# Reading the moving weights of the token-major products from the last column to the first

## The chip, the core and the metric

The kernel runs on one core of one Trainium2 chip. The time is that of the device for one execution of the whole program, in microseconds. The other cores of the chip have no work.

## What is computed

Two transformer blocks run one after the other on an activation `x` of 256 tokens by 2048 features, all in float32. Each block has a mixer and a feed-forward part. The attention and the recurrence are cut here, because the change touches none of their instructions.

```python
def first_block(x, ...):
    h = rms_norm(x, pre_mix_norm)
    proj = h @ w_in                       # 2048 x 5656
    mix = attention_of(proj)              # differential heads and compressed, selected and windowed heads
    x = x + rms_norm(mix @ w_out, post_mix_norm)
    h = rms_norm(x, pre_ffn_norm)
    u = causal_dwconv(h @ w_up, conv_w, conv_b)          # 2048 x 11264
    gate, up = jnp.split(u, 2, axis=-1)
    y = (jax.nn.gelu(gate, approximate=True) * up) @ w_down   # 5632 x 2048
    return x + rms_norm(y, post_ffn_norm)

def second_block(x, ...):
    proj = rmsnorm(x, mix_pre_gain) @ w_in_2             # 2048 x 5376
    mixed = concatenate([window_attention(proj), recurrence(proj)]) @ w_out_2
    x = x + rmsnorm(mixed, mix_post_gain)
    u = relu(rmsnorm(x, mlp_pre_gain) @ w_up_2)          # 2048 x 8192
    return x + rmsnorm((u * u) @ w_down_2, mlp_post_gain)
```

## The kernel before

Every large matrix product streams its weights from HBM once. A tile of weights is 512 KB, 128 partitions by 1024 float32 columns. SyncE brings it into one of eight slots of `stage`. ScalarE copies it to `whi` (lines 732, 790, 983, 1134), which rounds it to the type float32r, and VectorE subtracts that from the original and writes the rest to `wlo` (lines 1198, 1226, 1629, 1837). Both have four slots. The activations are kept in the same two parts, high in columns 0 to 255 and low in columns 256 to 511 of each chunk of 128 features. A product is the sum of three partial ones: high by high, high by low and low by high.

A matmul of TensorE holds a stationary operand of 128 by 128 in the array and streams a moving operand past it, one column after the other. Each column of the moving operand makes one column of the output in PSUM. The kernel has two kinds of products:

- **Feature-major** (`in1` and `in2` in part, `up1a`, `up1b`, `up2a`, `up2b`; lines 2097 and 2100, 2368 and 2371, 2024 and 2028): the weights are stationary, the activations move. The output has features on its partitions.
- **Token-major** (`in1` and `in2` in part, `out1`, `out2`, `down1a`, `down1b`, `down2a`, `down2b`): the activations are stationary, and the weights move. The output has 128 tokens on its partitions and up to 512 features in a bank of PSUM. The three partial products of one chunk follow each other, `ah` by `h`, `ah` by `l`, `al` by `h`, all into the same bank. They are lines 1911 to 1913 in `chunk`, 2113 to 2115 in `tok_tile`, and 2381 to 2383 in `in2_tile`. In most of them a weight tile holds two chunks of 512 columns (`NW`); some blocks of the input projections are 256 or 280 columns wide.

TensorE waits with `lo_done` until VectorE has written the whole of a tile of `wlo`, and gives the slot back with `tile_used` after the last matmul that reads it. So neither of these semaphores knows in which order the columns of a tile are read. Sixteen chunks of 128 rows make one sum for an input or output projection; the down projections sum over more. The order of all products is written out by hand in the program of each engine, and no planner moves anything.

On the host, `kernel` hands each input to the program as it is.

Of the kernel before, what the change touches and what calls it, by code (L numbers as in the profile page):

```python
# [17 lines left out]
D = 2048  # L18
S = 256
TT = S // P  # L20
KC = D // P
# [32 lines left out]
NW = 512  # L54
TC = TILE // NW
# [5 lines left out]
IN2_BLOCKS = [("tok", C_KA, 256)] + [("feat", C_QA + 256 * i, 256) for i in range(4)]  # L61
for _i in range(4):
# [13 lines left out]
IN1_BLOCKS = [("feat", C_KC, 256), ("feat", C_VC, 256), ("feat", C_KS, 256), ("feat", C_KW, 256),  # L76
              ("tok", C_VS, 256), ("feat", C_NQ, 256), ("tok", C_VW, 256 + GATES)]
# [48 lines left out]
def in2_block(n):  # L126

    k = max(k for k in range(len(IN2_BLOCKS)) if IN2_FIRST[k] <= n)
    return k, n - IN2_FIRST[k]
# [74 lines left out]
def build(nc, w, out, scratch, roots):  # L204
# [4 lines left out]
    def ev(name):  # L209

        if name not in sems:
            sems[name] = ctx.enter_context(nc.semaphore(name))
        return sems[name]

    with ctx:
# [81 lines left out]
        spans = win[:, 2048:4096]  # L297
# [135 lines left out]
        def region1_width(n):  # L433

            if n >= IN1_TILES:
                return TILE
            kind, _, wd = IN1_BLOCKS[in1_block(n)[0]]
            return TILE if kind == "feat" else TC * wd
# [54 lines left out]
        def _(sp):  # L493
# [5 lines left out]
            def tok_block(name, i, b, base):  # L499

                m, k0 = WT[name]
                col, _, _, wd = place(name, i, b)
                for j in range(G[name].tiles):
                    k = k0 + TC * j
                    slot = (b * G[name].tiles + j) % STAGES
                    tile_in(slot, base + j, m[k * P:(k + TC) * P, span(col, wd)].rearrange("(c p) n -> p c n", p=P),
                            stage[:, slot, 0:TC * wd].rearrange("p (c n) -> p c n", c=TC))
# [1396 lines left out]

        @block.tensor
        def _(pe):
            def chunk(o, lhs, k, s, c, t, ends):

                h, l = whi[:, s, c * NW:(c + 1) * NW], wlo[:, s, c * NW:(c + 1) * NW]
                ah, al = lhs[:, k, t * P:(t + 1) * P], lhs[:, k, S + t * P:S + (t + 1) * P]  # L1910
                nc.tensor.matmul(o, ah, h, start=k == 0, stop=False)  # L1911
                nc.tensor.matmul(o, ah, l, start=False, stop=False)  # L1912
                return nc.tensor.matmul(o, al, h, start=False, stop=ends and c == TC - 1)  # L1913

            def held_tiles(name, lhs, base):

                T = G[name].tiles
                for t in range(TT):
                    for j in range(T - HELD, T):
                        if t == 0:  # L1920
                            pe.wait_ge(ev("lo_done"), base + (j + 1 + STAGES))
                        for c in range(TC):
                            last = chunk(PS[:, LAST_BANK[name] + t, :], lhs, TC * j + c, (base + j) % SPLITS, c, t, j == T - 1)
                        if t == 1:
                            last.then_inc(ev("tile_used"), 1)
                    if t == 0:
                        last.then_inc(ev("half_tile"), 1)
# [26 lines left out]
            def last_chunks(turn):  # L1954

                n = {"n2": 0, "n3": 1, "n4": 2}[turn]
                pe.wait_ge(ev("actlo_" + turn), 4)
                turn_chunks(turn, range(12, KC))
                pe.wait_ge(ev("resid"), PIECES * n + 6)
                turn_chunks(turn, range(12, KC), t=1)  # L1960
# [144 lines left out]
            def tok_tile(bank, s, wd, first):  # L2105

                for c in range(TC):
                    at_k = first + c
                    h, l = whi[:, s, c * wd:(c + 1) * wd], wlo[:, s, c * wd:(c + 1) * wd]
                    for t in range(TT):  # L2110
                        o = PS[:, bank + t, 0:wd]
                        ah, al = act1[:, at_k, t * P:(t + 1) * P], act1[:, at_k, S + t * P:S + (t + 1) * P]
                        nc.tensor.matmul(o, ah, h, start=at_k == 0, stop=False)  # L2113
                        nc.tensor.matmul(o, ah, l, start=False, stop=False)  # L2114
                        last = nc.tensor.matmul(o, al, h, start=False, stop=at_k == KC - 1)  # L2115
                return last

            def out1_here(n):

                b, q = out1_tile(n)  # L2120
                if q == 0:
                    if b == 0:
                        pe.wait_ge(ev("in1_join"), len(IN1_FEAT))
                    if b == 1:
                        pe.wait_ge(ev("in1_tok"), 2 * len(IN1_TOK))
                    if b == 3:
                        pe.wait_ge(ev("actlo_mix1"), KC)
                    if b == 2:
                        pe.wait_ge(ev("diff_o"), HD)
                        pe.wait_ge(ev("actlo_mix1"), HN + 4)  # L2130
                if b < 2:
                    pe.wait_ge(ev("actlo_mix1"), TC * (q + 1))
                pe.wait_ge(ev("lo_done"), n + 1 + STAGES)
                tok_tile(2 * (b % 2) + 4 * (b // 2), n % SPLITS, NW, TC * q).then_inc(ev("tile_used"), 1)
# [209 lines left out]
            def in2_tile(n):  # L2344

                k, j = in2_block(n)
                kind, _, wd = IN2_BLOCKS[k]
                banks, s = IN2_BANKS[k], n % SPLITS
                if j == 0 and k == 14:
                    pe.wait_ge(ev("in2_join"), FEAT_NO[12] + 1)  # L2350
                elif j == 0 and k > 14:
                    pe.wait_ge(ev("in2_tok"), 2 * TOK_NO[k - 2] + 2)
                elif k < 14 and j == 0 and k >= 2:
                    if k - 2 in FEAT_NO:
                        pe.wait_ge(ev("in2_join"), FEAT_NO[k - 2] + 1)
                    else:
                        pe.wait_ge(ev("in2_tok"), 2 * TOK_NO[k - 2] + 2)
                if k == 0 and j == 2:
                    last_chunks("n3")
                if k == 0:  # L2360
                    pe.wait_ge(ev("actlo_n3"), TC * (j + 1))
                pe.wait_ge(ev("lo_done"), G["in2"].first + n + 1 + STAGES)
                if kind == "feat":
                    for c in range(FC):
                        at_k = FC * j + c
                        for f in range(2):
                            o, at = PS[:, banks[f], :], slice(c * FW + f * P, c * FW + (f + 1) * P)
                            nc.tensor.matmul(o, whi[:, s, at], act2[:, at_k, :], start=at_k == 0, stop=False)  # L2368
                        for f in range(2):
                            o, at = PS[:, banks[f], :], slice(c * FW + f * P, c * FW + (f + 1) * P)  # L2370
                            last = nc.tensor.matmul(o[:, S:2 * S], wlo[:, s, at], act2[:, at_k, 0:S], start=False, stop=at_k == KC - 1)  # L2371
                else:
                    for t in range(TT):
                        if t == 1 and j == 0 and k >= 14:
                            pe.wait_ge(ev("in2_tok"), 2 * TOK_NO[k - 1] + 1)
                        for c in range(TC):
                            at_k = TC * j + c
                            h, l = whi[:, s, c * wd:(c + 1) * wd], wlo[:, s, c * wd:(c + 1) * wd]
                            o = PS[:, banks[t], 0:wd]
                            ah, al = act2[:, at_k, t * P:(t + 1) * P], act2[:, at_k, S + t * P:S + (t + 1) * P]  # L2380
                            nc.tensor.matmul(o, ah, h, start=at_k == 0, stop=False)  # L2381
                            nc.tensor.matmul(o, ah, l, start=False, stop=False)  # L2382
                            last = nc.tensor.matmul(o, al, h, start=False, stop=at_k == KC - 1)  # L2383
                        if t == 0 and j == 7 and k >= 13:
                            last.then_inc(ev("first_half"), 1)
                last.then_inc(ev("tile_used"), 1)
# [161 lines left out]
        "mlp_pre_gain_2", "mlp_post_gain_2", "w_up_2", "w_down_2"]  # L2548


# [19 lines left out]
```

## Time and profile before

| | us |
|---|---|
| median of three runs | 2238.51 |
| lowest and highest run | 2238.21, 2238.97 |
| span of the profiled execution | 2235.6 |
| TensorE matmul busy | 2215.5 (99%) |
| TensorE weight load busy | 1891.4 (85%) |
| VectorE busy | 1416.2 (63%) |
| ScalarE busy | 1118.0 (50%) |

The span goes from the first to the last instruction of the profiled execution. It is 2.9 us shorter than the median of the runs, and no device time beside its span is recorded for that execution itself. In the profile, matmuls are pipelined and their ends are modelled: two of them overlap in the trace, so the duration of one says less than the distance from the start of one to the start of the next. Where this text speaks of a matmul's spacing, it is that distance.

### The profile page before, as it was taken

Reading aid. Unit: us, or ns where it says so; the run is one execution under the profiler, and the core shown is the slowest. Engines: PE = TensorE matmul, PEld = TensorE weight load, DVE = VectorE, ACT = ScalarE, POOL = GpSimd, SP = SyncE. Lnnn points to the kernel's source line nnn. Section 1 sums busy time; section 2 is a strip of 40 time slices with the busy share of each in tenths; the row PEclk is TensorE's granted clock in tenths of the full one; section 3 lists DMA queues with packets and bytes.
Section 4 is the critical chain, followed back from the end, with each engine's and each line's share of the span. In section 5 each row is a group of like instructions: output and inputs, shape, how many; then the busy total and the mean of one; then the engine's idle time right before and its main releaser. Section 6 shows DMA issues by size and latency. Waiting matters only on the chain.

```text
span 2235.6 us, 34152 instructions
## 1 busy us (share of the span) xinstructions
PE 2215.5 (99%) x12721; PEld 1891.4 (85%) x12721; DVE 1416.2 (63%) x1827; ACT 1118.0 (50%) x1567; POOL 65.7 (3%) x95
## 2 busy tenths in 40 slices
PE   8999999999999999999999999999999999999998
PEld 7888888888888888888888888888888888888887
DVE  6466685677776447777566786657666444666545
ACT  5454464555555445555454554545444444444443
POOL 5100000000000000000000000000000000000000
PEclk9999999999999999999999999999999999999999
DMA  9954455566566666666657455566666666666663
GB/s 291 317 180 133 132 167 181 162 190 205 178 201 195 190 194 189 187 188 200 209 147 206 142 162 160 180 195 167 196 191 193 191 196 190 191 192 188 214 192 112
DMA packets 321663, 418.84 MB, mean 187 GB/s; under 512 B 13566, under 2 KB 233048, under 8 KB 320788
## 3 DMA queue, kind: packets, MB, share of 16 engines
q1 hardware_dynamic: 316548, 398.81, 58.3%
q0 software_dynamic: 4720, 16.49, 2.5%
q10 hardware_dynamic: 288, 2.10, 0.3%
q8 instruction: 69, 1.13, 0.2%
q14 instruction: 38, 0.31, 0.0%
HBM read 414.85 MB, written 2.49 MB: 187 GB/s over the span
## 4 chain that ended last, share of the span: by engine, by line
PE 95%; DVE 2%; DMA 1%; issue 1%; ACT 1%; POOL 0%; POOLq 0%; DVEq 0%; SPq 0%; ACTq 0%
PE PS L2024 25%; PE PS L2028 13%; PE PS L1912 10%; PE PS L1911 10%; PE PS L1913 10%; PE PS L2097 5%; PE PS L2368 3%; PE PS L2100 2%; PE PS L2113 2%; PE PS L2115 2%; PE PS L2114 2%; PE PS L2371 2%; PE PS L2381 1%; PE PS L2383 1%; PE PS L2382 1%
## 5 line engine op out<-in xcount | busy, mean ns | idle before, releaser
L2024 PE MATMUL PS<-actu,whi 128*128 128x512 f32 x2432 | 755.6, 392 | 0.0
L2028 PEld LDWEIGHTS PS<-actu,wlo 128*128 128x128 f32 x2432 | 457.1, 188 | 99.9
L1226 DVE TENSOR_TENSOR wlo<-stage,whi 128x1024 fp32r<-128x1024 f32 x296 | 360.4, 1223 | 216.5 <-ACT whi L790 216.2
L1198 DVE TENSOR_TENSOR wlo<-stage,whi 128x1024 fp32r<-128x1024 f32 x245 | 298.9, 1225 | 301.2 <-ACT whi L732 301.2
L2028 PE MATMUL PS<-actu,wlo 128*128 128x256 f32 x2432 | 480.0, 279 | 0.0
L790 ACT ACTIVATE whi<-stage 128x1024 fp32r<-128x1024 f32 x296 | 311.4, 1057 | 304.9 <-PE PS L2028 291.6
L732 ACT ACTIVATE whi<-stage 128x1024 fp32r<-128x1024 f32 x245 | 258.7, 1060 | 344.6 <-PE PS L1913 321.4
L2024 PEld LDWEIGHTS PS<-actu,whi 128*128 128x128 f32 x2432 | 368.4, 188 | 0.6 <-issue 0.4
L1913 PE MATMUL PS<-whi,gT 128*128 128x512 f32 x864 | 336.4, 389 | 0.0
L1912 PE MATMUL PS<-wlo,gT 128*128 128x512 f32 x864 | 336.4, 389 | 0.0
L1911 PE MATMUL PS<-whi,gT 128*128 128x512 f32 x864 | 336.4, 389 | 0.0
L1629 DVE TENSOR_TENSOR wlo<-stage,whi 128x1024 fp32r<-128x1024 f32 (+2 forms) x125 | 145.3, 1166 | 109.0 <-ACT whi L983 108.7
L983 ACT ACTIVATE whi<-stage 128x1024 fp32r<-128x1024 f32 (+2 forms) x125 | 125.8, 1010 | 150.0 <-PE PS L2100 79.8
L1911 PEld LDWEIGHTS PS<-whi,gT 128*128 128x128 f32 x864 | 162.3, 188 | 33.8
L1913 PEld LDWEIGHTS PS<-whi,gT 128*128 128x128 f32 x864 | 162.2, 188 | 33.6
L1912 PEld LDWEIGHTS PS<-wlo,gT 128*128 128x128 f32 x864 | 162.2, 188 | 33.2
L2097 PE MATMUL PS<-act,whi 128*128 128x512 f32 x512 | 164.5, 403 | 0.0
L1837 DVE TENSOR_TENSOR wlo<-stage,whi 128x1024 fp32r<-128x1024 f32 (+1 forms) x86 | 102.9, 1204 | 62.4 <-ACT whi L1134 61.8
L1134 ACT ACTIVATE whi<-stage 128x1024 fp32r<-128x1024 f32 (+1 forms) x86 | 89.3, 1044 | 90.0 <-PE PS L2371 45.6
L2368 PE MATMUL PS<-act,whi 128*128 128x512 f32 x384 | 122.5, 400 | 0.1
L2100 PEld LDWEIGHTS PS<-act,wlo 128*128 128x128 f32 x512 | 96.3, 188 | 22.6
L2100 PE MATMUL PS<-act,wlo 128*128 128x256 f32 x512 | 101.0, 279 | 0.0
(338 smaller groups left out, 2482.4 us busy)
## 6 DMA issues: line engine op xcount, KB each, us to landing
stage<-in_w_up SPq DMA_DIRECT2D x304, 512.0 KB, 3.9
stage<-in_w_down SPq DMA_DIRECT2D x216, 512.0 KB, 4.2
stage<-in_w_in SPq DMA_DIRECT2D x160, 512.0 KB, 3.8
stage<-in_w_out SPq DMA_DIRECT2D x64, 512.0 KB, 4.2
stage<-in_w_in SPq DMA_DIRECT2D x16, 256.0 KB, 4.0
DQK<-in_cmp_k_w POOLq DMA_DIRECT2D x8, 512.0 KB, 6.6
DQK<-in_cmp_v_w POOLq DMA_DIRECT2D x8, 512.0 KB, 6.3
stage<-in_w_in SPq DMA_DIRECT2D x8, 280.0 KB, 8.3
```

Of the source, the lines that this page charges most:

```text
L732: nc.scalar.activation(whi[:, s % SPLITS, 0:wd], stage[:, s % STAGES, 0:wd], ACT.Copy)\
L790: nc.scalar.activation(whi[:, j % SPLITS, :], stage[:, j, :], ACT.Copy).then_inc(ev("hi_done"), 1)
L1198: nc.vector.tensor_tensor(wlo[:, s % SPLITS, 0:wd], stage[:, s % STAGES, 0:wd], whi[:, s % SPLITS, 0:wd].bitcast(F32), ALU.subtract).then_ ...
L1226: nc.vector.tensor_tensor(wlo[:, j % SPLITS, :], stage[:, j, :], whi[:, j % SPLITS, :].bitcast(F32), ALU.subtract).then_inc(ev("lo_done"), 1)
L1911: nc.tensor.matmul(o, ah, h, start=k == 0, stop=False)
L1912: nc.tensor.matmul(o, ah, l, start=False, stop=False)
L1913: return nc.tensor.matmul(o, al, h, start=False, stop=ends and c == TC - 1)
L2024: nc.tensor.matmul(o, whi[:, j % SPLITS, at], actu[:, k, :], start=k == 0, stop=False)
L2028: last = nc.tensor.matmul(o[:, S:2 * S], wlo[:, j % SPLITS, at], actu[:, k, 0:S], start=False, stop=k == KC - 1)
L2097: nc.tensor.matmul(o, whi[:, s, at], act1[:, at_k, :], start=at_k == 0, stop=False)
L2100: last = nc.tensor.matmul(o[:, S:2 * S], wlo[:, s, at], act1[:, at_k, 0:S], start=False, stop=at_k == KC - 1)
L2368: nc.tensor.matmul(o, whi[:, s, at], act2[:, at_k, :], start=at_k == 0, stop=False)
```

## The change

In the three places where weights move, the moving operand is now given with a step of minus one: the access pattern starts at the last column of the chunk and runs to the first. So that each output column still lands where it did, the host turns round the order of the columns of each block in the weight matrices. Column 511 of a chunk in SBUF now holds what column 0 held. The outputs in PSUM are written from column 0 upwards, as before. In `w_in` and `w_in_2` only the token-major blocks are turned; `w_up` and `w_up_2` are left as they are.

```diff
+            def falling(ap):
+
+                return ap[:, ::-1]
+
             def chunk(o, lhs, k, s, c, t, ends):
...
-                nc.tensor.matmul(o, ah, h, start=k == 0, stop=False)
-                nc.tensor.matmul(o, ah, l, start=False, stop=False)
-                return nc.tensor.matmul(o, al, h, start=False, stop=ends and c == TC - 1)
+                nc.tensor.matmul(o, ah, falling(h), start=k == 0, stop=False)
+                nc.tensor.matmul(o, ah, falling(l), start=False, stop=False)
+                return nc.tensor.matmul(o, al, falling(h), start=False, stop=ends and c == TC - 1)
...
+def moving_last_first(name, a):
+
+    if name in ("w_out", "w_out_2", "w_down", "w_down_2"):
+        spans = [(at, at + NW) for at in range(0, D, NW)]
+    elif name in ("w_in", "w_in_2"):
+        spans = [(col, col + wd) for kind, col, wd in (IN1_BLOCKS if name == "w_in" else IN2_BLOCKS) if kind == "tok"]
+    else:
+        return a
+    a = a.copy()
+    for at, end in spans:
+        a[:, :, at:end] = a[:, :, at:end][:, :, ::-1].copy()
+    return a
...
-        a = np.ascontiguousarray(inputs[name])
+        a = moving_last_first(name, np.ascontiguousarray(inputs[name]))
```

`tok_tile` and the token-major branch of `in2_tile` are edited like `chunk`. The sequence of instructions on every engine, their sizes, their waits and all transfers are the same before and after; the program gives each of these matmuls as one instruction, as before. The output arrays and their layout are unchanged.

## Rows read from the trace of the kernel before

**Rows 1.** The page: span, busy time by engine, granted clock and DMA in 40 slices.
```profile
span 2235.6 us, 34152 instructions
PE 2215.5 (99%) x12721; PEld 1891.4 (85%) x12721; DVE 1416.2 (63%) x1827; ACT 1118.0 (50%) x1567; POOL 65.7 (3%) x95
...
PEclk9999999999999999999999999999999999999999
DMA  9954455566566666666657455566666666666663
...
PE 95%; DVE 2%; DMA 1%; issue 1%; ACT 1%; POOL 0%; POOLq 0%; DVEq 0%; SPq 0%; ACTq 0%
```

**Rows 2.** Waits of TensorE: whom it waited for, us in total, times, longest us.
```profile
PE PS L2049 <- DMA ident<-const_ident: 6.6, 1, 6.6
PE PS L1934 <- DVE x L1360: 3.3, 5, 1.1
```

**Rows 3.** Groups by line and shape: count, busy us, mean ns, idle before us.
```profile
L1911 PE MATMUL PS<-whi,gT 128*128 128x512 f32 x864 | 336.4, 389 | 0.0
L2113 PE MATMUL PS<-whi,act 128*128 128x512 f32 x176 | 69.7, 396 | 0.0
L1911 PE MATMUL PS<-whi,act 128*128 128x512 f32 x144 | 56.2, 390 | 0.0
L2381 PE MATMUL PS<-whi,act 128*128 128x512 f32 x128 | 50.9, 398 | 0.0
L2113 PE MATMUL PS<-whi,act 128*128 128x280 f32 x32 | 9.6, 298 | 0.0
L2113 PE MATMUL PS<-whi,act 128*128 128x256 f32 x32 | 9.3, 289 | 0.0
L2381 PE MATMUL PS<-whi,act 128*128 128x256 f32 x32 | 9.2, 289 | 0.3 <-DVE act L1323 0.3
```

**Rows 4.** Timeline of TensorE in a token-major stage: start us, duration us, instruction.
```profile
754.74 0.39 PE L1911 MATMUL PS<-whi,gT 128*128 128x512 f32 x1
754.97 0.39 PE L1912 MATMUL PS<-wlo,gT 128*128 128x512 f32 x1
755.19 0.39 PE L1913 MATMUL PS<-whi,gT 128*128 128x512 f32 x1
...
757.91 0.39 PE L1913 MATMUL PS<-whi,gT 128*128 128x512 f32 x1
```

**Rows 5.** Timeline of TensorE in the 280-column block of the first input projection.
```profile
94.43 0.29 PE L2113 MATMUL PS<-whi,act 128*128 128x280 f32 x1
...
96.50 0.29 PE L2114 MATMUL PS<-wlo,act 128*128 128x280 f32 x1
```

**Rows 6.** Timeline of TensorE around a product of plain float32 operands (L2237).
```profile
182.53 0.59 PE L2237 MATMUL PS<-work,VS 128*128 128x256 f32 x2
182.96 0.38 PE L2238 MATMUL PS<-work,VS 128*128 128x128 f32 x2
```

**Rows 7.** Lines 2450 and 2467: duration ns min/median/max, first and last start us.
```profile
L2450 PE MATMUL PS<-win x128: 218/219/244, 1335.4 to 1337.2; 128*32 128x64 f32 x128
...
L2467 PE MATMUL PS<-win x32: 221/222/270, 1377.4 to 1378.3; 128*64 128x64 f32 x32
```

**Rows 8.** Timelines of ScalarE and VectorE in down2a, with the idle time before each.
```profile
1751.56 1.06 ACT L732 ACTIVATE whi<-stage 128x1024 fp32r<-128x1024 f32 x1 [1.66 <-PE PS L1913]
...
1752.66 1.23 DVE L1198 TENSOR_TENSOR wlo<-stage,whi 128x1024 fp32r<-128x1024 f32 x1 [1.50 <-ACT whi L732]
1755.38 1.23 DVE L1198 TENSOR_TENSOR wlo<-stage,whi 128x1024 fp32r<-128x1024 f32 x1 [1.50 <-ACT whi L732]
```

**Rows 9.** Stage by window, down2a: engines' busy us (count), granted clock, DMA share, GB/s.
```profile
1702.40:1876.30 173.90, 173.90 (x770) 144.08 (x769) 82.89 (x68) 72.62 (x72) 0.00 (x0) 1.00 0.63 193
```

**Rows 10.** DMA issues: count, KB each, median us from issue to landing.
```profile
stage<-in_w_down SPq DMA_DIRECT2D x216, 512.0 KB, 4.2
```

**Rows 11.** Timeline of TensorE in a feature-major stage.
```profile
1000.16 0.62 PE L2024 MATMUL PS<-actu,whi 128*128 128x512 f32 x2
1000.62 0.40 PE L2028 MATMUL PS<-actu,wlo 128*128 128x256 f32 x2
1000.85 0.62 PE L2024 MATMUL PS<-actu,whi 128*128 128x512 f32 x2
```

More of the change, by code:

```diff
@@ L2112, in tok_tile @@
                         ah, al = act1[:, at_k, t * P:(t + 1) * P], act1[:, at_k, S + t * P:S + (t + 1) * P]
-                        nc.tensor.matmul(o, ah, h, start=at_k == 0, stop=False)
-                        nc.tensor.matmul(o, ah, l, start=False, stop=False)
-                        last = nc.tensor.matmul(o, al, h, start=False, stop=at_k == KC - 1)
+                        nc.tensor.matmul(o, ah, falling(h), start=at_k == 0, stop=False)
+                        nc.tensor.matmul(o, ah, falling(l), start=False, stop=False)
+                        last = nc.tensor.matmul(o, al, falling(h), start=False, stop=at_k == KC - 1)
                 return last
@@ L2380, in in2_tile @@
                             ah, al = act2[:, at_k, t * P:(t + 1) * P], act2[:, at_k, S + t * P:S + (t + 1) * P]
-                            nc.tensor.matmul(o, ah, h, start=at_k == 0, stop=False)
-                            nc.tensor.matmul(o, ah, l, start=False, stop=False)
-                            last = nc.tensor.matmul(o, al, h, start=False, stop=at_k == KC - 1)
+                            nc.tensor.matmul(o, ah, falling(h), start=at_k == 0, stop=False)
+                            nc.tensor.matmul(o, ah, falling(l), start=False, stop=False)
+                            last = nc.tensor.matmul(o, al, falling(h), start=False, stop=at_k == KC - 1)
                         if t == 0 and j == 7 and k >= 13:
```

## The prediction

> **What bounds the kernel now.** I read the page first, then the waits of TensorE, then the groups by line and shape, then the timelines of single stages. The page gives TensorE 99% busy and 95% of the chain that ended last, at a granted clock of 9 tenths or more in all 40 slices [rows 1]; in the stage that I look at most closely it is 1.00, so the level of 2.4 GHz [rows 9]. TensorE waited 6.6 us once for the first transfer, and then hardly again: the next entry of its list is 3.3 us in five waits [rows 2]. So no engine feeds it too slowly, and the time is the sum of the spacings of its matmuls. A change to the matmuls' own speed reaches the end one to one, and nothing else does.
>
> The token-major products are 4,224 matmuls. Lines 1911 to 1913 have 864 + 144 each, so 3,024 in all; lines 2113 to 2115 have 176 + 32 + 32 each, so 720; lines 2381 to 2383 have 128 + 32 each, so 480 [rows 3]. Of these 3,936 are 512 columns wide (3 x 864, 3 x 176, 3 x 144 and 3 x 128), 96 are 280 wide and 192 are 256 wide.
>
> Their spacing is very regular. From 754.74 to 757.91 us lie 14 spacings, so one is 226.4 ns [rows 4]. At 2.4 GHz 512 columns take 213.3 ns, which leaves 13.1 ns per matmul. For 280 columns, 16 spacings fill 94.43 to 96.50 us, so 129.4 ns against 116.7 ns: 12.7 ns are left [rows 5]. In a feature-major stage two matmuls of 512 and two of 256 columns take 1000.85 - 1000.16 = 0.69 us [rows 11], against 1,536 columns / 2.4 = 640 ns: 12.5 ns per matmul. So a matmul of this type costs its columns at full rate plus about 13 ns, whichever operand moves and however wide it is. Of the span, token-major products fill 3,936 x 0.2264 + 96 x 0.1294 + 192 x 0.120 (256 / 2.4 + 13 ns) = 891 + 12 + 23 = 926 us, or 41%. The other 59% is not touched.
>
> **The change, part by part.**
>
> *Data and transfers.* The host turns the columns in DRAM, the tiles have the same shape and size, and a weight tile lands in 4.2 us as before [rows 10]. The copy to `whi` and the difference for `wlo` work column by column, and don't care what a column holds. Cost: none. The numbers that TensorE multiplies are the same, only in other places of SBUF.
>
> *Waits.* TensorE now begins a tile with the column that was written last. But it waits for the whole tile of `wlo`, and so no semaphore has to move. The cover is ample too: in down2a VectorE works 1.23 us and then idles 1.50 us for each tile, ScalarE works 1.06 and idles 1.66 us [rows 8], and the DMA engines are 63% busy [rows 9]. Nothing is released earlier or later, because the last matmul on a slot is the same one. Cost: none.
>
> *The step of minus one on 4,224 moving operands.* This is the whole question, and the trace of before has no operand that is read downwards. So I bound it on both sides by the nearest rows.
>
> Towards the gain, the most that can vanish is the part of a spacing that is not columns: 13 ns x 4,224 = 55 us, for a total of 2183.5. I see no reason why the direction should remove it. The feature-major matmuls pay the same 12.5 ns with quite other operands, and it doesn't depend on the width.
>
> Towards the loss, there are two prices. One is a fixed cost at each start, if the address has to be set up in another way or the first line is fetched too late to hide. The nearest size for that is what a start costs today, 13 ns once more: 55 us. The other is a lower rate. The trace has a row for a stream that takes its columns at half the rate: line 2237 multiplies plain float32, and its two records of 256 columns take 182.96 - 182.53 = 0.43 us, 0.215 us each [rows 6], which is 0.84 ns a column. If a downward read fell to this rate, a matmul of 512 columns would take 0.43 us, 0.204 more: x 3,936 = 803 us. The 96 of 280 columns would take 0.235 instead of 0.129 (10 us more), the 192 of 256 0.215 instead of 0.120 (18 us more). Together 831 us, and a total of 3069.
>
> What do other rows say of unusual moving operands? Line 2450 moves 64 columns that lie in two pieces of 32, far apart in SBUF, and line 2467 moves 64 columns in one piece. The two-piece records last 219 ns, the one-piece ones 222 ns [rows 7]. A break of the address in the middle of a stream costs nothing that can be seen. And in the 280-column block the second chunk starts at column 280 of the tile, the first at column 0, and all the spacings are alike [rows 5]. These rows are the nearest to the change: where a stream begins and where it jumps doesn't matter. They don't show a negative step, and line 2450 runs at the half rate of plain float32, so they would not show an access that is only good for half of the full rate. I take 0 ns per matmul, and keep 13 ns more as the end of the likely cases.
>
> The Trainium skill, in "Advanced Engine Details and Errata", section "Memory Cachelines", says that SBUF has lines of 16 bytes, and that a stream with at least two hits on each line has its full rate. Four-byte columns read downwards hit each line four times, as upwards; by that rule the sum is unchanged at 2238.5, and the half rate doesn't come. No run here shows the rule for a falling read of TensorE.
>
> *The writes to PSUM.* They rise as before and go to the same banks, three partial products in a row to one bank. If they fell in one matmul and rose in the next, the last column written would be needed at once; here nothing of that kind changes. Cost: none.
>
> The sum is 2235.6 + 0 for the profiled execution; its span lies 2.9 us under the median of the runs, and with these the forecast is 2238.5.
>
> **The rivals.**
>
> *A start that costs more (slower).* If each falling stream needs a few ns more before its first column, at each of the 4,224 matmuls, it reaches the end in full, since TensorE is never late for anything else. The price is 4.2 us for each nanosecond: 2242.7 with 1 ns, 2293.5 with 13 ns. It decides against "no change" from 1.1 ns (4.5 us, 0.2% of the time). For it speaks that starts aren't free today. Against it, the evenness of the spacings whatever the start and whatever the width.
>
> *Half rate (slower).* 3069, as worked out above. For it speaks that the full rate moves four bytes per column at 2.4 GHz, while plain float32 is served at half of that; a port that reads two neighbouring columns at once would do so only upwards, if it was built simply. Against it: a fetch of aligned pairs or lines serves either direction. The price decides from any loss of rate above 0.5% of the columns' time (4.5 us of the 891).
>
> *The start gets cheaper (faster).* If the 13 ns are the wait for the first columns of a rising stream, and a falling one avoids that, up to 55 us go: 2183.5. From 1.1 ns on it can be measured. VectorE and ScalarE would keep up, with 1.5 us idle in a tile that would be 12 x 13 ns = 0.16 us shorter [rows 8]. Against it speaks that the moving activations and the moving weights pay the same.
>
> The Trainium skill, in "TensorE: Matmul & The Clock Gate", section "Back-to-back issue gap", gives columns / 2.4 + 2.5 ns for a single matmul's gap, so 215.8 ns for 512 columns. The row shows 226.4, so the trace disagrees by 10.6 ns; were the falling read to reach the page's gap, 4,224 x 10.6 = 45 us would go, for 2194.
>
> *The change doesn't do what it says.* Turned data read in turned order might be made into a rising read somewhere, and then the time is that of before. In the program each of these matmuls has a moving operand with the step -1, so I count this with "no change", and give it no chance of its own.
>
> **How the numbers follow.** No change 0.64; a dearer start 0.14; half rate 0.12; a cheaper start 0.10. The predicted time is that of the likeliest, 2238.5. Its own range is 2234 to 2243, about 0.2% each way, which is what a measurement of this kernel can tell from no change. For 8 in 10 the range takes in the dearer start up to one more start of today's size (2293.5, rounded up to 2296) and the small part of a cheaper start down to 2230 (2 ns per matmul). Half rate, at 3069, and the rest of the cheaper start stay outside, some 0.2. Faster by over 0.2%: 0.10. Within 0.2%: 0.64. Slower: 0.14 + 0.12 = 0.26.
>
> **What would show it.** In the profile of the changed kernel, the spacing of lines 1911 to 1913 would stay at 226 ns, and down2a would fill 173.9 us [rows 9]. A dearer start shows as the same addition to 256, 280 and 512 columns; a lower rate shows as an addition that grows with the width. Feature-major stages must keep their 0.69 us for four matmuls, and TensorE's list of waits must stay as short as it is. If VectorE or ScalarE had other durations on the token-major tiles, my step on the data would be wrong. If TensorE's granted clock left 1.00, something outside of this argument would be at work.

## The result: 24 us slower, all of it in the 512-column products

| | before | after |
|---|---|---|
| median us | 2238.36 (4 runs) | 2262.77 (4 runs) |
| lowest and highest run | 2238.06, 2238.97 | 2262.17, 2263.38 |
| span of the profiled execution | 2235.6 | 2260.5 |

The ratio is 1.0109, with a 95% interval of 1.0095 to 1.0123. The change costs 24.4 us. That lies inside the range, but "no change" was wrong.

The page of the kernel after, first, with the lines that answer to [rows 1]:

```profile
span 2260.5 us, 34152 instructions
PE 2240.4 (99%) x12721; PEld 1890.3 (84%) x12721; DVE 1417.0 (63%) x1827; ACT 1119.2 (50%) x1567; POOL 65.8 (3%) x95
...
PEclk9999999999999999999999999999999999999999
```

TensorE is busy 24.9 us longer, and the span grew by 24.9 us. VectorE and ScalarE have what they had, the counts of instructions are the same, and the granted clock did not move. TensorE's waits, for [rows 2], stay small too: 5.8 us for the first transfer, and at most 2.8 us in total for any other entry.

```profile
PE PS L2053 <- DMA ident<-const_ident: 5.8, 1, 5.8
PE PS L1938 <- DVE x L1360: 2.8, 5, 0.9
```

The stages tell where the time went. This is down2a by window, for [rows 9], and the feature-major stage up2b behind it:

```profile
1717.10:1896.20 179.10, 179.10 (x770) 144.32 (x769) 82.86 (x68) 72.75 (x72) 0.00 (x0) 1.00 0.62 188
1896.30:2072.90 176.60, 176.60 (x1025) 155.42 (x1024) 110.48 (x92) 82.08 (x80) 0.00 (x0) 1.00 0.64 190
```

down2a takes 179.1 us in place of 173.9, so 5.2 us or 6.8 ns for each of its 768 matmuls. up2b has this row before:

```profile
1876.50:2053.00 176.50, 176.50 (x1024) 155.46 (x1023) 110.45 (x92) 81.95 (x80) 0.00 (x0) 1.00 0.63 190
```

So the feature-major stage is untouched. The timeline of TensorE in the kernel after, in a down stage, is to be read beside [rows 4]:

```profile
755.12 0.40 PE L1917 MATMUL PS<-whi,gT 128*128 128x512 f32 x1
755.36 0.40 PE L1915 MATMUL PS<-whi,gT 128*128 128x512 f32 x1
755.59 0.40 PE L1916 MATMUL PS<-wlo,gT 128*128 128x512 f32 x1
...
757.92 0.40 PE L1917 MATMUL PS<-whi,gT 128*128 128x512 f32 x1
```

Twelve spacings fill 2.80 us: 233.3 ns each, where 226.4 was read before, alike for all three lines. But in the 256-column block the spacing is no longer than it was. These rows are of the kernel after, then of the kernel before:

```profile
65.73 0.28 PE L2118 MATMUL PS<-wlo,act 128*128 128x256 f32 x1
...
66.92 0.28 PE L2119 MATMUL PS<-whi,act 128*128 128x256 f32 x1
```

```profile
65.74 0.28 PE L2114 MATMUL PS<-wlo,act 128*128 128x256 f32 x1
...
66.94 0.28 PE L2115 MATMUL PS<-whi,act 128*128 128x256 f32 x1
```

Ten spacings: 1.19 us after, 1.20 before. So it is not one addition per start. Nor is it a loss of rate in proportion to the columns: that would put some 3.4 ns on a 256-column matmul, half of the 6.9 at 512. Whatever it is depends on the width in another way. Summed over all starts in the two traces, the 3,936 spacings at 512 columns come to 25.0 us more, 6.4 ns each; the 96 at 280 columns to 0.1 us more and the 192 at 256 columns to 0.2 us less. That is the 24.9 us of the span.

### The profile page after: what moved, and what is told of

The parts are those of the page before. It is cut to its first block, busy times and chain, and to the rows that moved or that the text cites. A ratio compares the mean times of both kernels' runs of the same rounds, so it can differ in the third digit from the quotient of the medians.

```text
span 2260.5 us, 34152 instructions
## 1 busy us (share of the span) xinstructions
PE 2240.4 (99%) x12721; PEld 1890.3 (84%) x12721; DVE 1417.0 (63%) x1827; ACT 1119.2 (50%) x1567; POOL 65.8 (3%) x95
## 4 chain that ended last, share of the span: by engine, by line
PE 95%; DVE 2%; DMA 1%; issue 1%; ACT 1%; POOL 0%; POOLq 0%; DVEq 0%; ACTq 0%
PE PS L2028 25%; PE PS L2032 12%; PE PS L1915 10%; PE PS L1917 10%; PE PS L1916 10%; PE PS L2101 5%; PE PS L2372 3%; PE PS L2104 2%; PE PS L2117 2%; PE PS L2118 2%; PE PS L2119 2%; PE PS L2375 2%; PE PS L2385 1%; PE PS L2386 1%; PE PS L2387 1%
## 5 line engine op out<-in xcount | busy, mean ns | idle before, releaser
L1226 DVE TENSOR_TENSOR wlo<-stage,whi 128x1024 fp32r<-128x1024 f32 x296 | 360.4, 1224 | 215.8 <-ACT whi L790 215.5
L1916 PE MATMUL PS<-wlo,gT 128*128 128x512 f32 x864 | 343.4, 397 | 0.0
L1915 PE MATMUL PS<-whi,gT 128*128 128x512 f32 x864 | 343.3, 397 | 0.0
L1917 PE MATMUL PS<-whi,gT 128*128 128x512 f32 x864 | 343.3, 397 | 0.0
```

Source lines behind the costliest of these rows:

```text
L1226: nc.vector.tensor_tensor(wlo[:, j % SPLITS, :], stage[:, j, :], whi[:, j % SPLITS, :].bitcast(F32), ALU.subtract).then_inc(ev("lo_done"), 1)
L1915: nc.tensor.matmul(o, ah, falling(h), start=k == 0, stop=False)
L1916: nc.tensor.matmul(o, ah, falling(l), start=False, stop=False)
L1917: return nc.tensor.matmul(o, al, falling(h), start=False, stop=ends and c == TC - 1)
```

## The experiments

### One part alone: the data, and one matmul of three

```diff
 # e1_data_only: the columns stay turned on the host
-                return ap[:, ::-1]
+                return ap
```

> The kernel after with the columns turned on the host and the moving operands read upwards as in the kernel before, so that the token-major outputs come out in turned order. Theory A, B and C (the cost sits in the direction of the read): 2238.4 us, as before, spacing 226.4 ns. Theory D (the turned data, by other values next to each other, cost the 24.4 us): 2262.8.

Measured: 2237.69 us (10 runs), beside 2237.73 for the kernel before; ratio 1.0001, interval 0.9992 to 1.0011. The turned data cost nothing that can be measured here, so theory D is out. The cost sits in the direction of the read.

```diff
 # e2_low_falls: in the three places, against the kernel after
-                nc.tensor.matmul(o, ah, falling(h), start=k == 0, stop=False)
+                nc.tensor.matmul(o, ah, h, start=k == 0, stop=False)
                 nc.tensor.matmul(o, ah, falling(l), start=False, stop=False)
-                return nc.tensor.matmul(o, al, falling(h), start=False, stop=ends and c == TC - 1)
+                return nc.tensor.matmul(o, al, h, start=False, stop=ends and c == TC - 1)
```

> The kernel after with only the second of the three matmuls (the one that moves wlo) read downwards; the first and third read upwards. The columns of the high and low part then don't fit each other, which leaves the sums of the token-major products wrong, with the same instructions. Theory A: a third of the cost, 8.1 us, so 2246.5, and only the matmul that falls has the longer spacing. If the cost sits in the turn from one direction to the other rather than in the direction, two of three spacings carry it: 2254.6 or more. If it sits in falling after falling, nothing is left: 2238.4.

Measured: 2245.62 us against 2237.73, ratio 1.0034 (1.0020 to 1.0048). That is 7.9 us, a third of 24.4. By the starts in its trace, in the products with `gT`, the falling matmul has a mean of 232.5 ns to the next start, and the two rising ones 226.7 and 227.6. So it is the falling matmul's own cost, not one of changing the direction.

### Widths, directions and traffic in a program of its own

A small program shows what a whole kernel hides. It loads four tiles, splits them as the kernel does, and then TensorE runs one block of 96 matmuls after another, each on a line of its own:

```python
# 512 down
for r in range(8):
    for c, t in ((0, 0), (0, 1), (1, 0), (1, 1)):
        for k, (a, m) in enumerate(trio(512, c, t, r, 0)):   # (ah, h), (ah, l), (al, h)
            nc.tensor.matmul(PS[:, t, 0:512], a, down(m), start=k == 0, stop=k == 2)
```

> A program of its own: it loads 4 tiles, splits them in the high and low part as the kernel does, and then TensorE alone runs blocks of 96 matmuls in the order of a token-major tile (high, low, high), one block on each source line, widths 64 to 512, rising and falling, and some at 512 with other patterns. The attention, the products and everything else of the kernel are left out. The kernel's own two traces gave for a spacing 226.4 ns rising and 233.2 ns falling at 512 columns, 120 and 118.3 at 256. Theory A (two prices of the stream itself: a start some 10 ns cheaper, each column 0.032 ns dearer): the same numbers here, and on a line between them at other widths, so at 384 about 173 rising and 175.8 falling, at 128 about 67 and 61. Theory B (a fixed price that a stream pays once it is longer than some width): equal or cheaper up to that width, and then a step that stays the same; 512 and 448 would carry the same addition. Theory C (the falling read meets the writes of VectorE, ScalarE or the transfers in SBUF): with TensorE alone falling and rising are the same, 226 at 512.

> The same blocks, with ScalarE copying and VectorE subtracting tiles of 1024 columns without a pause, and SyncE bringing in tiles of 512 KB beside, all in tensors of their own. What they compute is used by nothing. Theory A and B: every block as in m1_alone. Theory C: falling at 512 columns is 233 or more here and 226 alone, since the traffic is denser than in the kernel.

Of the program alone, the view of a line gives the first and last start of its high matmuls. A block's first and last matmul are both high, so 95 spacings lie between them. First 512 columns rising and falling, then 256 rising and falling, then 256 of plain float32 rising and falling (192 records, two for a matmul):

```profile
L198 PE MATMUL PS<-whi,act x64: 388/394/404, 272.2 to 294.1; 128*128 128x512 f32 x64
...
L204 PE MATMUL PS<-whi,act x64: 394/397/399, 294.3 to 316.5; 128*128 128x512 f32 x64
...
L150 PE MATMUL PS<-whi,act x64: 276/280/300, 148.3 to 159.5; 128*128 128x256 f32 x64
...
L156 PE MATMUL PS<-whi,act x64: 278/282/286, 159.6 to 170.9; 128*128 128x256 f32 x64
...
L270 PE MATMUL PS<-raw,fx x192: 378/379/379, 540.9 to 582.1; 128*128 128x256 f32 x192
L276 PE MATMUL PS<-raw,fx x192: 379/379/379, 582.3 to 623.5; 128*128 128x256 f32 x192
```

Falling takes 22.2 / 95 = 233.7 ns, as in the kernel. But rising takes 21.9 / 95 = 230.5 and not 226.4, and the durations spread from 388 to 404 ns. So the rising stream, which I had taken for the fixed point, is the one that varies. By the starts of single matmuls the mean was 231.0 ns rising and 233.4 falling at 512 columns, 202.5 and 205.9 at 448, 175.1 and 176.8 at 384, 146.6 and 146.8 at 320, 118.0 and 118.9 at 256. Theory B's one step from some width on isn't there: falling takes 0.9, 0.2, 1.7, 3.4 and 2.4 ns more at 256, 320, 384, 448 and 512 columns. Plain float32 takes 41.2 / 191 = 215.7 ns a record either way: in that type direction doesn't matter. (Most of the blocks of 64 and 128 columns ran at a granted clock of 0.50, so the level of 1.2 GHz, and tell nothing here.)

With ScalarE and VectorE at work and transfers coming in, the same two lines read:

```profile
L198 PE MATMUL PS<-whi,act x64: 388/394/404, 272.0 to 293.9; 128*128 128x512 f32 x64
...
L204 PE MATMUL PS<-whi,act x64: 394/397/399, 294.1 to 316.3; 128*128 128x512 f32 x64
```

They are the same to 0.1 us. Theory C, that the stream meets the traffic of the other engines, is out. Theory A fails as well: it asked for 226 ns rising at 512.

Other blocks of m1_alone answer three more questions. With each of the three matmuls in another bank of PSUM, falling takes 233.4 ns, and rising 231.4 when one single gap of 418 ns is left out: the bank is not the cause. With the two halves of the chunk swapped and each read upwards, so that a rising stream jumps once, it takes 231.4; with each half read downwards, 233.5. So a jump in the middle costs next to nothing even at full rate, and the direction within each piece counts. And with every second column read, 256 columns over a chunk of 512, a matmul takes almost as long as the whole chunk:

```profile
L246 PE MATMUL PS<-whi,act x64: 390/420/427, 451.9 to 473.6; 128*128 128x256 f32 x64
```

That is 21.7 / 95 = 228.4 ns rising, and 233.5 falling, against 118 for 256 columns that lie side by side. Half the rate exists in this program, then, but for a step of two columns and not for a falling one.

What differs between the slots? In this program a slot is 4160 bytes long, 64 more than a multiple of 256; in the kernel it is 4096. Sorted by slot, the rising spacings have medians of 227, 230, 232 and 233 ns in slots 0 to 3, and the same in the block with one and the same stationary operand. That led to the next theory: the distance in SBUF between the moving and the stationary operand.

### The distance between the two operands

> TensorE alone as in m1_alone, but every block now reads the same two tiles, which start at a fixed place. What differs from block to block is the start of the moving operand (0, 16, 32, 64, 128, 192 or 256 bytes further on) or of the stationary one; the last blocks have the order of a feature-major tile. In m1_alone rising blocks of 512 columns took 226 to 241 ns, by the slot of the tile, and the slots start 4160 bytes apart, which is 64 more than a multiple of 256. Theory E (the stream of the moving operand and the load of the next stationary operand meet in SBUF, and how often depends on the distance of their addresses and on whether they run in opposite directions): a rising block of 512 columns takes about 226.5 at distance 0 and 233 at another one; 256 bytes further gives the same as 0; moving both by 64 bytes gives the same as 0; falling takes 233 at 0 and has another value at another distance. Theory A (two prices of the falling stream itself): rising 226.5 at each distance that keeps the start on 16 bytes, falling 233 at each. Theory F (only the place of the moving operand counts, not the distance): moving both by 64 bytes gives the value of the moving one moved by 64, and moving the stationary alone changes nothing.

Measured, by the starts of single matmuls, mean of each block of 96 at 512 columns:

| moving operand further on by | 0 | 16 | 32 | 64 | 128 | 192 | 256 bytes |
|---|---|---|---|---|---|---|---|
| rising, ns | 226.7 | 231.6 | 233.4 | 228.9 | 232.3 | 233.4 | 227.1 |
| falling, ns | 233.4 | 233.5 | 233.4 | 233.4 | 233.3 | 233.3 | 233.4 |

Both operands 64 bytes on: rising 227.2, falling 233.4. Only the stationary one 64 bytes on: rising 233.3, which is the value at 192 bytes. The lines of four rising blocks, at distance 0, at 192 bytes, with both 64 bytes on, and with the stationary operand alone 64 bytes on:

```profile
L119 PE MATMUL PS<-whi,act x64: 389/389/389, 47.9 to 69.4; 128*128 128x512 f32 x64
...
L149 PE MATMUL PS<-whi,act x64: 393/396/402, 158.5 to 180.7; 128*128 128x512 f32 x64
...
L203 PE MATMUL PS<-whi,act x64: 389/389/398, 359.6 to 381.2; 128*128 128x512 f32 x64
...
L215 PE MATMUL PS<-whi,act x64: 393/393/398, 403.8 to 425.9; 128*128 128x512 f32 x64
```

They take 21.5, 22.2, 21.6 and 22.1 us for 95 spacings: 226.3, 233.7, 227.4 and 232.6 ns. So for a rising stream in this order of matmuls the distance of the two operands modulo 256 bytes decides, to within 1 ns, and not the place of one of them. That is the first half of theory E's forecast; F and A are out. That moving stream and weight load meet in SBUF, which theory E gives as the reason, is not shown by it. The second half, that a falling stream has other values at other distances, is not so: it takes 233.3 to 233.5 everywhere here.

Now the result has a shape. In the kernel before, `whi`, `wlo`, `act1`, `act2`, `gT1` and `gT2` all start at multiples of 256 bytes. Its token-major products read at distance 0, the cheapest case that any run here shows at 512 columns, and they got there by the order in which tensors were allocated. A falling read gives that up.

### The same in the kernel, without any falling read

If that is right, the kernel before must get as slow as the kernel after when its weights are moved a little.

```diff
 # e4_before_moved (kernel before) and e3_after_moved (kernel after)
-        stat = sb("stat", [P, 2, 16])
         stage = sb("stage", [P, STAGES, TILE])
         whi = sb("whi", [P, SPLITS, TILE], F32R)
         wlo = sb("wlo", [P, SPLITS, TILE], F32R)
+        stat = sb("stat", [P, 2, 16])
```

> The kernel before, with nothing turned, and one small tensor (stat, 128 bytes in each partition) allocated behind wlo instead of ahead of stage, so that stage, whi and wlo start 128 bytes earlier, and all the activations stay where they were. The moving weights of the token-major products now start 128 bytes from their stationary operand (modulo 256), where before they started at distance 0. Theory E (the distance decides how often moving stream and weight load meet), with the prices of m3_phase: 3,936 matmuls of 512 columns x (232.3 - 226.7) = 22 us, and in the up projections distance 64 becomes 192, 4,864 matmuls x (173.9 - 173.3) = 3 us: some 2263 us, about the time of the kernel after, with every read rising. Theory A (only a falling read costs): 2238.4.

Measured: 2264.02 us against 2237.60, ratio 1.0119 (1.0102 to 1.0136). Expected was 2263. The timeline of the token-major products in the moved kernel:

```profile
1759.92 0.40 PE L1911 MATMUL PS<-whi,gT 128*128 128x512 f32 x1
1760.15 0.39 PE L1912 MATMUL PS<-wlo,gT 128*128 128x512 f32 x1
...
1763.41 0.39 PE L1911 MATMUL PS<-whi,gT 128*128 128x512 f32 x1
```

Fifteen spacings fill 3.49 us: 232.7 ns, with all reads rising.

> The kernel after with the same move of 128 bytes. Theory E, by m3_phase: a falling stream of 512 columns takes 233.4 ns at each distance, so the token-major products stay as they are, and only the up projections pay their 3 us: some 2265.5 us. If the move cost something of its own, which has nothing to do with rising streams (the split by ScalarE and VectorE, or the transfers), it would come on top here as in e4_before_moved: 2287.

Measured: 2276.35 us against 2237.60, ratio 1.0172 (1.0155 to 1.0189). That is 11 us more than expected. The move does cost the falling kernel something: its products with `gT` have these starts:

```profile
1759.61 0.40 PE L1915 MATMUL PS<-whi,gT 128*128 128x512 f32 x1
...
1761.97 0.40 PE L1916 MATMUL PS<-wlo,gT 128*128 128x512 f32 x1
```

Ten spacings fill 2.36 us, 236 ns; the mean over all 2,592 is 236.9, 3.6 ns above the 233.3 of the small program. With 2,592 of them that is 9 of the 11 us. The falling 512-column products with `act`, at the same distance, have a mean of 233.9 ns (gaps over 300 ns left out). So falling isn't the same at every distance, nor in every product at one distance.

```diff
 # e5_before_64 (kernel before)
+        parts = sb("parts", [P, TT, 8])
         stage = sb("stage", [P, STAGES, TILE])
...
-        parts = sb("parts", [P, TT, 8])
```

> The kernel before, with nothing turned, and another small tensor (parts, 64 bytes) moved ahead of stage, so that whi and wlo start 64 bytes later and the activations stay. Token-major products get distance 64 instead of 0: 3,936 x (229.0 - 226.7) = 9 us by m4_scan; the up projections get 0 instead of 64: 4,864 x (174.6 - 173.1) = 7 us; the feature-major blocks of the input projections 192 instead of 0: 1,792 x (173.9 - 174.6) = 1 us less. Theory E: 2238 + 15 = 2253 us, so between the kernel before and the one moved by 128 bytes. If any move away from distance 0 costs the same, 2264. If the 24 us of e4_before_moved came from something else that depends on the 128 bytes, 2238.

Measured: 2252.94 us against 2237.43, ratio 1.0067 (1.0050 to 1.0084). The sum of block prices from the small program gave 2253. By the starts in the trace, the down products have a mean of 229.2 ns (expected 229.0), with medians of 232, 226 and 229 ns for lines 1911, 1912 and 1913; the small program's block at 64 bytes has the same three values in another order. The up products take 8.0 us more (expected 7), and the feature-major blocks of the input projections 0.4 us more, where 1 us less was expected; that term was too small to be tested. The single terms missed by up to 1.4 us and in part made up for each other. Still, a price list from a program of its own told the time of the whole kernel to within 1 us at a place where it had not been run. This is the run that convinces me most.

### All distances, and the width of the stationary operand

> TensorE alone as in m3_phase: rising blocks of 512 columns, of 256, and feature-major ones, each at 16 distances from 0 to 240 bytes in steps of 16; then 512 columns with a stationary operand of 128, 64 and 32 columns, rising at distance 0 and 128 and falling at 0. Theory E: the values at 0, 16, 32, 64, 128 and 192 are those of m3_phase, the others lie between 224 and 234, and the additions shrink with the stationary operand, since the load is shorter: falling 233.4 at 128 columns, about 230 at 64 and 228 at 32, if the meeting happens during the load. If the addition has nothing to do with the load, falling stays 233.4 at each width. Open: whether there is a distance under 226.7, which a faster kernel could use.

Measured at 16 distances, rising, mean ns of a block:

| bytes | 0 | 16 | 32 | 48 | 64 | 80 | 96 | 112 | 128 | 144 | 160 | 176 | 192 | 208 | 224 | 240 |
|---|---|---|---|---|---|---|---|---|---|---|---|---|---|---|---|---|
| 512 columns | 226.7 | 231.6 | 233.4 | 233.3 | 229.0 | 231.0 | 233.4 | 231.1 | 232.5 | 233.2 | 234.2 | 231.1 | 233.3 | 234.7 | 233.3 | 226.7 |
| 256 columns | 119.8 | 118.7 | 116.7 | 118.3 | 117.8 | 120.0 | 120.0 | 113.3 | 118.6 | 118.7 | 117.3 | 119.3 | 113.5 | 119.2 | 118.3 | 117.2 |

For feature-major tiles the mean over their four matmuls was 174.6 at 0, lowest at 64 bytes (173.1), highest at 208 (177.8). No distance beats 226.7 at 512 columns. The up projections of the kernel before already stand at 64 bytes, and its token-major products at 0. The best place for the 256-column blocks (113.3) would bring 192 x 6.5 ns = 1.2 us, too little to be told from nothing. The feature-major blocks of the input projections stand at 0, and at 64 they would save 1,792 x 1.5 ns = 2.7 us, by the small program; but they read the same `act1` and `act2` as the token-major blocks, which are best at 0. So the experiments point to no version clearly faster than the kernel before, and I ran none.

The width of the stationary operand went against theory E. Rising at distance 0: 227.1 ns with 128 stationary columns, 230.1 with 64, 231.7 with 32. Falling: 233.3 with each of the three. Two of these falling blocks, with 128 and with 32 columns:

```profile
L419 PE MATMUL PS<-whi,act x64: 396/397/398, 986.1 to 1008.3; 128*128 128x512 f32 x64
...
L455 PE MATMUL PS<-whi,act x64: 395/395/395, 1119.4 to 1141.6; 128*32 128x512 f32 x64
```

22.2 us each, though the record of a weight load fell from 188 to 108 ns. A shorter weight load doesn't make the falling stream cheaper, and makes the best rising one dearer. So the addition doesn't follow the length of the load, as theory E had asked. Rising at 128 bytes goes the other way: 233.3 ns with 128 stationary columns, 229.3 with 64 and 230.7 with 32, so with narrow stationary operands 128 bytes is slightly better than 0. Which distance is good depends on the width of the load, and of the two distances tried none came down to 227 ns with a narrow one. That is a description, not a cause.

### What was left of the moved falling kernel

> TensorE alone, with the weights and activations at the very addresses of e3_after_moved: high and low weights in four slots, activations at the place of act1 (actA) or of gT1 (actG), 8 chunks in turn. e3_after_moved had 236.7 ns for a falling stream with gT1 and about 234 with act1, where m3_phase gave 233.3 for each distance. Theory E1 (beyond the distance, the place itself counts modulo 256 bytes): falling, moving at 128 and stationary at 0 takes 236.7 with one chunk and one slot too, and 233.3 the other way round, moving at 0 and stationary at 128, which was the case of m3_phase. Theory E2 (the change of chunk and slot counts): 233.3 with one chunk and one slot, 236.7 with all of them. Either way, falling with moving at 0 and stationary at 0 takes 233.3, rising 226.7, and rising at 128 takes 232.4, as in the kernels. The last 16 blocks give falling streams at 16 distances; by m3_phase nothing there lies under 233.

Measured: falling, moving at 128 and stationary at 0, 236.6 ns with `actG` and `actA` alike, 236.7 with one chunk and one slot, and 236.6 too with moving at 0 and stationary at 128. Falling at distance 0: 233.3. With both at 128, which is distance 0 again, falling takes 233.3 and rising 226.8, as with both at 0. The lines of falling at 0 and at 128:

```profile
L133 PE MATMUL PS<-W,actG x96: 396/397/398, 93.8 to 116.0; 128*128 128x512 f32 x96
...
L140 PE MATMUL PS<-W,actG x96: 398/400/400, 116.2 to 138.7; 128*128 128x512 f32 x96
```

So the price of the moved kernel's products with `gT` is reproduced with TensorE alone, but neither E1 nor E2 explains why m3_phase had 233.3 at the same distance. One thing that still differs is how far the high and low tensors lie apart: 18,432 bytes there and 16,384 here for the weights, 2,560 and 1,024 for the activations. Whether that is the reason was not tested. So the distance modulo 256 is not all that counts. Of 16 distances for a falling stream here, 14 took 233.3 or 233.4, and 128 and 240 took 236.6. None lies below. Rising at 128 took 233.3 here and 232.3 there. That small a difference says nothing of the layout: m4_scan has two blocks with the same instructions at the same addresses, and they took 232.5 and 233.3. Nor does this program give the products with `act` of e3_after_moved: `actA` stands at their very place and takes 236.6, and they took 233.9.

## Why the prediction was wrong, step by step

**What bounds the kernel**: right. TensorE's spacings make the time, and 24.9 us more of busy time came out as 24.9 us more of span.

**Data, transfers, waits, PSUM**: right at no cost. e1_data_only shows it for the data. In down2a VectorE and ScalarE have the durations of [rows 8], and idle a little longer.

**The step of minus one**: this is the step that failed. I took 0 ns per matmul; it was 6.4 ns for the 3,936 of 512 columns (25.0 us), 1.4 ns for the 96 of 280, and 1 ns less for the 192 of 256. I had two reasons for 0, and neither carries it.

The first was that start and jump don't matter, by the 280-column block, whose two chunks start at different places with alike spacings [rows 5], and by line 2450 [rows 7]. The jump is right: m1_alone shows 231.4 ns with the halves swapped, against 231.0. The start is not. The second chunk starts 280 x 4 = 1,120 bytes on, which is 96 modulo 256. In the scan with 256 columns, 0 and 96 bytes happen to take 119.8 and 120.0 ns, whereas at 512 columns they are 226.7 and 233.4. In the trace of the kernel before, the two chunks of the 280-column block have means of 128.1 and 129.4 ns (gaps over 200 ns left out). The row was true, and nearly blind by luck of that distance and width. The two rows on line 2450 and line 2467 compare durations, and I had said myself that the spacing is what counts: 128 records of the one start within 1.8 us and 32 of the other within 0.9, so a duration of 219 or 222 ns tells nothing of what a jump costs. And line 2450 works on plain float32, where m1_alone finds no difference of direction at all. I had written that reservation down myself and then didn't let it weigh.

The second was the evenness of the spacings [rows 4]. I read it as a fixed cost of 13 ns that nothing influences. It was the sign of one fixed relation of addresses, held in every tile, and of the best one that the runs found. The 12.5 ns of the feature-major matmuls [rows 11] were a mean over two widths: by the starts in the trace of before, the 512-column ones with `actu` take 229.4 ns and the 256-column ones 115.8, so 16 and 9 ns beyond their columns. It was not the same addition at each width even there. The profile had a second hint: in the feature-major stages the 512-column matmuls with `act` took 233 ns at the median and those with `actu` 229. `actu` starts 64 bytes off the 256-byte grid; in e5_before_64, where its distance from the weights becomes 0, they take 233.

**The rivals.** "A start that costs more" had the right sign and a size inside its price: 24.4 us over 4,224 matmuls are 5.8 ns each. But its mechanism, the same addition at each width, isn't what the timeline shows; that the wide range took in the measured time is luck in so far, since it was drawn for that mechanism. "Half rate" fell: 233.3 ns is far from 430, and the read that did come near half the rate was the one of every second column. "A start that gets cheaper" fell at 512 columns. Its small cousin is real, though: at 112 or 192 bytes a rising 256-column stream takes 113.3 to 113.5 ns.

**The rule of the Trainium skill** on lines of 16 bytes ("Advanced Engine Details and Errata", section "Memory Cachelines") asks only for two hits on each line, and by it neither direction nor distance would count. Here rising streams whose starts all lie on 16 bytes take 226.7 to 234.7 ns, so the rule does not give these times. The blocks of every second column hit each line twice and should by the rule keep the full rate; they take 228.7 and 233.5 ns for 256 columns, against 118.0 and 118.9 side by side. For the moving operand in float32r the measurements go against it. Nor did any 512-column block come down to the 215.8 ns that the prediction took for a single matmul from "TensorE: Matmul & The Clock Gate", section "Back-to-back issue gap".

## What stays open

Which part of the chip makes the 6 to 7 ns is not shown. Shown is that other engines and transfers have no share (m2_beside), nor has the bank of PSUM (m1_alone); that the relation of the moving and the stationary address counts for rising streams (m3_phase, e4_before_moved, e5_before_64); that no falling block of 512 columns had a mean under 233.3 ns; and that the addition doesn't follow the length of the weight load (m4_scan). Why a falling stream takes 236.6 at a distance of 128 in one layout and 233.3 in another is open too, and why the falling products with `act` in e3_after_moved take 233.9 where m5_places has 236.6.

## What to carry to other kernels

When TensorE is the bound and its matmuls stream float32r at full rate, note for each product the distance between its moving and its stationary operand modulo 256 bytes, and treat the order of allocations as part of the tuning: a tensor of 128 bytes put elsewhere moved this kernel by 26 us, more than the change under study. The good distance has to be measured for the order of matmuls and the widths at hand: it was 0 for token-major products of 512 columns, and 64 bytes for feature-major ones (m4_scan). A very even spacing doesn't prove that nothing influences it; it may be the best case of something that a change gives up. And a row bounds a new operation only if it has the same type, width and rate.

## What the runs showed of the chip that I had not expected

- The spacing of full-rate float32r matmuls with 512 moving columns depends on the distance of the two operands in SBUF, from 226.7 to 234.7 ns over 16 distances, with the same value at 0 and at 256 bytes to within 0.4 ns; 256 columns, from 113.3 to 120.0.
- A chunk that lies one column further on, so that its lowest column is off the 16-byte grid, costs more: in m1_alone 238.5 ns rising and 235.7 falling, against 231.0 and 233.4.
- Every second column of a float32r chunk takes about as long as the whole chunk: 228.7 ns rising and 233.5 falling for 256 columns, against 118.0 and 118.9 side by side.
- Read from the last column to the first, a 512-column stream takes 233.3 ns at 14 of 16 distances, and 236.6 at the other two.
- Plain float32 at half the rate takes 215.7 ns for a record of 256 columns in both directions.
